# Second block: head sums, spreads and decay rows in row and column groups, key products by head pairs, value projection first, blocks stored sooner

## The chip, the cores and the metric

One core of one Trainium2 chip runs the kernel. The metric is the device time of one execution in microseconds (us). Times are medians of runs; the profile is of one execution, taken by the hardware profiler. The engines are TensorE (PE, its weight loads PEld), VectorE (DVE), ScalarE (ACT), GpSimd (POOL) and SyncE, whose queue (SP) issues the DMAs.

## What is computed

Two transformer blocks, one after the other, on 256 tokens of width 1024, in fp32. The first block has two layers of mixers, cross attention and MLP. The second block has a hybrid mixer (a grouped-query attention beside a gated delta rule in both directions) and an expert layer of 16 experts. The change is within the hybrid mixer:

```python
proj = h @ w_in
aq, ak, av, dq, dk, dv, dz, b_raw, a_raw, g_raw = split(proj)
q = axial_rope(rmsnorm_2(heads(aq, 8), q_norm_w)); k = axial_rope(rmsnorm_2(heads(ak, 2), k_norm_w))
attn = block_attention(q, k, heads(av, 2))
cq, ck, cv = split(silu(short_conv(concat([dq, dk, dv]), conv_w)))
qd, kd = l2norm(heads(cq, 8)) * 64 ** -0.5, l2norm(heads(ck, 8))
beta, g = sigmoid(b_raw), -exp(a_log) * softplus(a_raw + dt_bias)
# both directions, each with chunks of 128 tokens, per head:
gc = cumsum(g)
decay = exp(where(incl, gc[:, None] - gc[None, :], -inf))
L = where(strict, (kd * beta) @ kd.T * decay, 0)
T = inverse(eye + L)
u, w = T @ (v * beta), T @ (kd * beta * exp(gc))
a_intra = where(incl, qd @ kd.T * decay, 0)
...
dn = rmsnorm_2(o_fwd + o_bwd, dn_norm_w) * silu(dz)
merged = sigmoid(gate_a) * (attn @ w_attn_up) + sigmoid(gate_d) * (dn @ w_dn_up)
x = x + gt1 * (merged @ w_o)
```

## The kernel before

The program writes out the order of each engine's work by hand; engines wait for each other by semaphores. Activations lie with features on the 128 partitions and the 256 tokens along the free axis, so two heads of 64 share a 128-row chunk. Dense weights come in units of 2 MB through a ring of six slots: `take()` on PE waits for the next unit's load, and SP issues a unit's load when the unit that had the slot has been read (`unit_read`). Eight PSUM banks: `fill(name, b)` takes a bank (without `b` the next of banks 0 to 3) and waits until its last content was freed; `mark` tells that it is filled, `full` waits for that on another engine, `copied` waits until the content was read. All PE products of `mm` have line 521 of the profile, all ScalarE work has line 1719. An fp32 product of the program is two matmul instructions.

The part of the mixer that matters, in PE's order before: `ba` (beta and decay inputs); projections `dq` and `aq`; `gc` (the cumulated decays with tokens on partitions); `head_sums` for l2 (sums of squares of each of 16 heads, one 128x16 product for each of eight chunks, all into 16 rows of one bank); `ak`; `head_spread` for l2 (each head's inverse root, a row of 16, spread over its 64 rows by products 16x64); `av`; then for each of eight heads `triangle(h)`: `kk` (keys by keys and queries by keys, four products 64x128 with 128 columns) and `gr` (the head's cumulated decay as a row, in all 128 partitions, four products 128x128 with 128 columns), with a quarter of the projections `dv` and `dz` after each head. Then the sums and spreads of the attention's q and k norm (`qn`), gates 0 to 2, the rotation products (`rotg`), and the attention (`gqa`), with gates 3 to 6 between its heads. After it come the merging of the inverses (`X5` to `TT6`), the states and outputs of the delta rule, the attention up-projection (`au`), with the sums and spread of the output norm (`on`) between its groups, and the down branch (`du`).

On DVE, `differences(h)` subtracts the decays, `triangle(h)` multiplies kk, decay and beta; four convolutions of the value channels lie between the heads. `store_blocks` on SP waits for the last two heads' kk to be read, stores the 32x32 diagonal blocks, and loads them back; DVE then solves all blocks at once by 31 steps of forward substitution (`substitute`, L3016 and L3018), nine before the rotations and the others (`solve`) between the heads of the attention. `load_inverses` on SP (L1578) waits for that, stores both forms of the inverses and loads them to their places. SP's queue is strictly in order: before, the blocks are stored after unit GATES_AT+1 was issued, and the inverses before unit GATES_AT+4. GATES_AT is the first unit of the gate projections; GATES_AT+3 holds gates 6 and 7, GATES_AT+4 the attention up-projection. Expert units follow all dense units in SP's queue, but for one that is loaded early; the last dense unit waits until PE has read `au3`.

Lines of the kernel before: `head_sums` L1242, `head_spread` L1250, PE's `triangle` L1269, `store_blocks` L1568, `load_inverses` L1578, ScalarE's `head_root` L2024, DVE's `differences` L2969 and `triangle` L2978, `substitute` L3012, `solve` L3031.

Of the kernel before, what the change touches and what calls it, by code (L numbers as in the profile page):

```python
# [13 lines left out]
P = 128  # L14
S = 256
# [98 lines left out]
def dense_units(a):  # L114
# [49 lines left out]
def program(nc, a, out, plan):  # L164

    ctx = ExitStack()
    with ctx:
# [114 lines left out]
        dk_shift, g16 = small(4), small(16)  # L282
# [173 lines left out]
        QROOT, QINV = rtp[0:16, 512:768], rtp[0:16, 768:1024]  # L456
# [29 lines left out]
        def _(pe):  # L486
# [746 lines left out]
            columns("aq", hT)  # L1233
# [16 lines left out]
            def head_spread(tag, order, inverse, count, b=None):  # L1250

                pe.wait_ge(inv_ready, count)
                for r in order:
                    ps = fill(f"{tag}{r}", None if b is None else b + r)
                    for j in range(2):
                        c = 2 * (2 * r + j)
                        for i in range(2):
                            last = mm(ps[half(i), j * S:(j + 1) * S], ident[0:16, c + i:c + i + 1].broadcast_to([16, HD]),
                                      inverse, True, True)
                    mark(last, f"{tag}{r}")  # L1260
# [8 lines left out]
            def triangle(h):  # L1269

                r, c = half(h), h // 2
                ps = fill(f"kk{h}", 4 + 2 * (h % 2))
                for t in range(TT):
                    tok = slice(t * P, (t + 1) * P)
                    mm(ps[:, t * P:(t + 1) * P], cv[r, 4 + c, tok], cv[r, 4 + c, tok], True, True)
                    last = mm(ps[:, (2 + t) * P:(3 + t) * P], cv[r, 4 + c, tok], cv[r, c, tok], True, True)
                mark(last, f"kk{h}")
                ps = fill(f"gr{h}", 5 + 2 * (h % 2))
                for d in range(2):
                    for t in range(TT):  # L1280
                        j = 2 * d + t
                        last = mm(ps[:, j * P:(j + 1) * P],
                                  gl[:, t, 8 * d + h:8 * d + h + 1].broadcast_to([P, P]), cum[:, d, :], True, True)
                mark(last, f"gr{h}")

            copied(pe, *(f"l2{r}" for r in range(4)))
            for i, tag in enumerate(("dv", "dz")):
                w, u = take()
                for c in range(4):
                    triangle(4 * i + c)  # L1290
                    b, j = divmod(c, 2)
                    if j == 0:
                        ps = fill(f"{tag}{b}")
                    for k in range(DC):
                        last = mm(ps[:, j * S:(j + 1) * S], w[:, k, c * P:(c + 1) * P], hT[:, k, :], k == 0, k == DC - 1)
                    if j:
                        mark(last, f"{tag}{b}", u=u if b else None)
# [1975 lines left out]
```

## Time and profile before

| | |
|---|---|
| median of 3 runs | 1628.72 us (1624.97 to 1629.79) |
| the profiled execution | 1628.91 us |
| its span, first to last instruction | 1627.1 us |
| granted TensorE clock, mean of the span | 0.952 of full speed |
| busy PE, PEld, DVE, ACT, POOL | 1470.3, 1147.7, 767.4, 293.1, 30.0 us |
| matmuls | 10036 |
| moved by DMA | 396.51 MB, mean 244 GB/s |

Busy time is the union of an engine's instructions. Matmuls are pipelined, so one instruction's duration (some 380 ns for 256 columns) is longer than the step from one start to the next; costs are therefore read from starts. A granted clock of 0.5 is TensorE's lower level. A stretch's DMA share is the mean busy share of the core's 16 DMA engines. The mixer of the second block runs from about 885 to 1137 us of the span, the expert layer from about 1165 us on.

### The profile page before, as it was taken

The numbers are of one execution on the slowest core, as the hardware profiler recorded it, in microseconds if no ns is written. First come the engines' busy times: TensorE is split into PE (matmuls) and PEld (weight loads), VectorE is DVE, ScalarE is ACT, GpSimd is POOL, SyncE is SP. The second block draws the span as 40 slices with busy tenths as digits, with TensorE's granted clock in tenths as the row PEclk, the third lists the DMA queues.
The fourth block names the chain that finished last, engine by engine and source line by source line (L and its number), as shares of the span: only waits on it lengthen the run. The fifth ranks groups of instructions, "written<-read, shape, count | busy, mean of one in ns | idle before, by whom it ended". The sixth has DMA issues, their size and how long they took to land.

```text
span 1627.1 us, 23549 instructions
## 1 busy us (share of the span) xinstructions
PE 1470.3 (90%) x10036; PEld 1147.7 (71%) x10036; DVE 767.4 (47%) x1564; ACT 293.1 (18%) x735; POOL 30.0 (2%) x51
## 2 busy tenths in 40 slices
PE   9999999999999999999999999999997656666665
PEld 8779989998897899899988887778853212213111
DVE  6538618778586565287876837823231000000000
ACT  1331012310043411223101322231010001000000
POOL 0000000000001000000000012000000000000000
PEclk9999999999999999999999999999999888888778
DMA  9525415866344154257773004233999999999998
GB/s 395 217 79 207 155 53 220 315 257 257 142 155 156 61 198 156 82 216 286 279 290 143 1 1 130 104 105 113 385 405 429 427 429 428 426 430 428 427 430 332
DMA packets 47176, 396.51 MB, mean 244 GB/s; under 512 B 16352, under 2 KB 20192, under 8 KB 22624
## 3 DMA queue, kind: packets, MB, share of 16 engines
q1 hardware_dynamic: 45600, 393.51, 60.4%
q8 instruction: 80, 1.31, 0.3%
q10 hardware_dynamic: 1472, 1.49, 0.3%
q14 instruction: 24, 0.20, 0.0%
HBM read 392.36 MB, written 2.63 MB: 243 GB/s over the span
## 4 chain that ended last, share of the span: by engine, by line
PE 76%; DMA 21%; SPq 1%; DVE 1%; ACT 0%; issue 0%; DVEq 0%; ACTq 0%
PE pb L521 34%; DMA arena<-in_w_experts 16%; PE pb L1086 12%; PE pb L1050 11%; PE pb L621 7%; DMA ring<-in_w_experts 5%; PE pb L961 5%; PE pb L994 3%; PE pb L1135 2%; PE pb L889 1%; PE pb L1161 1%; PE pb L692 1%; SPq L1660 1%; PE pb L750 0%; DMA cols<-in_cols 0%
## 5 line engine op out<-in xcount | busy, mean ns | idle before, releaser
L521 PE MATMUL pb<-hT,ring 128*128 128x256 f32 x768 | 175.3, 384 | 0.0
L521 PE MATMUL pb<-ring,hT 128*32 128x512 f32 (+2 forms) x704 | 117.3, 701 | 53.3 <-DMA ring<-in_w_experts 52.1
L521 PEld LDWEIGHTS pb<-hT,ring 128*128 128x128 f32 x768 | 144.3, 191 | 26.1 <-issue 7.5
L3182 DVE SCALAR_TENSOR_TENSOR side<-side,pb 128x256 f32<-128x256 f32 x16 | 6.7, 421 | 272.2 <-ACT side L1719 272.2
L521 PEld LDWEIGHTS pb<-ring,hT 128*32 128x32 f32 (+1 forms) x704 | 35.6, 138 | 121.2 <-issue 64.6
L621 PE MATMUL pb<-arena,ring 128*128 128x256 f32 x512 | 118.2, 382 | 0.0
L1719 ACT ACTIVATE arena<-pb 128x512 f32<-128x512 f32 (+4 forms) x124 | 54.8, 457 | 322.0 <-PE pb L521 125.8
L621 PEld LDWEIGHTS pb<-arena,ring 128*128 128x128 f32 x512 | 94.9, 190 | 14.6 <-issue 2.9
L1719 ACT ACTIVATE side<-pb 128x256 f32<-128x256 f32 (+2 forms) x58 | 23.1, 406 | 417.0 <-PE pb L521 400.8
L521 PE MATMUL pb<-arena,hT 128*32 128x512 f32 x248 | 41.9, 796 | 33.5 <-DMA arena<-in_w_experts 20.5
L521 PE MATMUL pb<-arena 128*64 128x128 f32 (+4 forms) x464 | 69.8, 331 | 0.8 <-ACT arena L1719 0.8
L521 PEld LDWEIGHTS pb<-arena 128*64 128x64 f32 (+2 forms) x464 | 49.5, 168 | 18.8 <-issue 13.8
L2519 DVE CUSTOM_DVE_ANT_0 ring<-ring,arena,cols 128x1024 f32<-128x1024 f32 x48 | 59.2, 1278 | 0.0
L1086 PE MATMUL pb<-ring,arena 128*128 128x256 f32 x256 | 58.2, 379 | 0.0
L1086 PE MATMUL pb<-arena,hT 128*128 128x256 f32 x256 | 57.9, 379 | 0.0
L1086 PE MATMUL pb<-ring,hT 128*128 128x256 f32 x256 | 57.9, 379 | 0.0
L3194 DVE TENSOR_TENSOR side<-pb,rstd 128x256 f32<-128x256 f32 x16 | 6.8, 425 | 107.3 <-PE pb L521 107.3
L521 PE MATMUL pb<-ring,side 128*32 128x256 f32 x576 | 43.8, 456 | 14.8 <-DMA ring<-in_w_experts 10.0
L1050 PE MATMUL pb<-hT,ring 128*128 128x128 f32 x448 | 54.6, 275 | 0.0
L521 PEld LDWEIGHTS pb<-arena,hT 128*32 128x32 f32 x248 | 7.4, 126 | 66.0 <-DMA arena<-in_w_experts 33.5
L1086 PEld LDWEIGHTS pb<-arena,hT 128*128 128x128 f32 x256 | 48.6, 190 | 6.6
L1086 PEld LDWEIGHTS pb<-ring,hT 128*128 128x128 f32 x256 | 48.6, 190 | 6.6
(463 smaller groups left out, 2522.8 us busy)
## 6 DMA issues: line engine op xcount, KB each, us to landing
ring<-in_w_dense SPq DMA_DIRECT2D x85, 2048.0 KB, 7.9
ring<-in_w_experts SPq DMA_DIRECT2D x56, 2048.0 KB, 44.9
arena<-in_w_experts SPq DMA_DIRECT2D x18, 2048.0 KB, 44.0
extra<-in_w_experts SPq DMA_DIRECT2D x10, 2048.0 KB, 44.4
arena<-in_w_experts SPq DMA_DIRECT2D x9, 1024.0 KB, 41.8
cons<-in_w_experts SPq DMA_DIRECT2D x9, 1024.0 KB, 44.6
ring<-in_w_dense SPq DMA_DIRECT2D x2, 1536.0 KB, 6.6
ring<-in_w_dense SPq DMA_DIRECT2D x4, 512.0 KB, 8.6
```

The source lines that it names most:

```text
L521: return nc.tensor.matmul(o, l, r, start=st, stop=sp)
L621: last = nc.tensor.matmul(proj["banks"][c // 2][:, (c % 2) * S:(c % 2 + 1) * S], w[:, k, (c % 4) * P:(c % 4 + 1) * P], yT[:, k, :], start= ...
L692: last = nc.tensor.transpose(ps[:, c:c + P], pr2[:, n % 4, qb, kb * P:(kb + 1) * P], ident)
L889: last = nc.tensor.matmul(ps[b][:, j * S:(j + 1) * S], w[:, k, (2 * b + j) * P:(2 * b + j + 1) * P], raw_x[:, k, :], start=k == 0 and j == ...
L961: last = nc.tensor.matmul(ps[b][:, o:o + P], lhs[x][:, k, f * P:(f + 1) * P], rhs[x][:, k, :], start=x in "156" and f == 0 and k == 0, sto ...
L994: last = nc.tensor.matmul(pv[j[0]][:, FEAT[j[1]]], rows_[l](k), cols_[r](k), start=k == 0 and n < 4, stop=k == 3, skip_group_check=True)
L1050: last = nc.tensor.matmul(ps[b][:, o:o + P], lhs[x][:, k, f * P:(f + 1) * P], rhs[x][:, k, :], start=x in "156" and f == 0 and k == 0, sto ...
L1086: last = nc.tensor.matmul(pq[j[0]][:, FEAT[j[1]]], rows_[l](k), cols_[r](k), start=g == 0 and k == 0 and n < 4, stop=g == 3 and k == 3, sk ...
L1135: last = nc.tensor.matmul(ps[b][:, o:o + P], lhs[x][:, k, f * P:(f + 1) * P], rhs[x][:, k, :], start=x in "156" and f == 0 and k == 0, sto ...
L1161: last = nc.tensor.matmul(pv[b][:, FEAT[side_]], rows_[l][:, k, :], cols_[r][:, k, :], start=k == 0 and n < 4, stop=k == 3, skip_group_che ...
L1719: return nc.scalar.activation(o, i, f, **kw)
L2519: ins = V.tensor_tensor_reduce(out=w, in0=w, in1=c_row, scale=1.0, scalar=col("b_ada", 4 * i + f), op0=ALU.mult, op1=ALU.add, accum_out=mo ...
```

## The change

Order of the units: the value unit (`dv`, column 1792) is loaded and used before `aq` (column 0) and `kv`. On PE:
- `gcrow`: eight products make the cumulated decays of all heads and both directions as rows, in partitions 0 to 15 and again in 64 to 79. ScalarE copies them to SBUF (`decays`). A head's row is then spread by two products of 16 rows with 256 columns, for two heads in turn, one at rows 0 to 15 and one at rows 64 to 79 (`decay_rows`), where each head had four products of 128 rows.
- `triangles(p, ...)`: kk of a pair of heads, one in rows 0 to 63 and one in rows 64 to 127, in turn.
- `head_sums`: each pair of chunks has its own 32 output rows (a column group), the first chunks of all pairs ahead of the second. `head_spread`: inverses lie in rows of 32 for each pair; products of 32 rows by 64, row groups in turn.
- The order becomes dq, half of dv, gc, gcrow, half of dv, then aq in quarters with the decay rows, l2 sums and spread between, then aq, ak with the triangles, av, dz in quarters with the qn sums and spread.

ScalarE gets a small Sqrt ahead of each head root and a small Exp after it (`warms`), and does the exponentials of the decays earlier. DVE does the differences before and around the l2 normalisation, then all triangles, then the convolutions of the values; substitution steps 0 to 5 stand before the rotations, 6 to 17 before the attention, 18 to 30 in four parts behind its first four heads (before: 0 to 8, then five parts). GpSimd waits for the normalised keys before its first product. SP stores the blocks after unit GATES_AT, and stores and loads the inverses before unit GATES_AT+3.

```diff
-    for c0 in (1280, 768, 0):
+    for c0 in (1280, 768, 1792, 0):
         unit(a["w_in_2"], 0, D, c0, 512)
     unit(a["w_kv_2"], 0, D, 0, 384)
-    for c0 in (1792, 2304):
-        unit(a["w_in_2"], 0, D, c0, 512)
+    unit(a["w_in_2"], 0, D, 2304, 512)
...
             columns("dq", hT)
-            columns("aq", hT)
...
+            w, u = take()
+            quarter("dv", w, 0)
+            quarter("dv", w, 1)
             pe.wait_ge(g_ready, 1)
             ps = fill("gc")
...
+            ps = fill("gcrow")
+            for d in range(2):
+                for t in range(TT):
+                    for e in range(2):
+                        at_ = (2 * d + t) * P
+                        last = mm(ps[HD * e:HD * e + NE, at_:at_ + P], gl[:, t, :], cum[:, d, :], True, True)
+            mark(last, "gcrow")
+            quarter("dv", w, 2)
+            quarter("dv", w, 3, u)
...
-                for i, (c, sq_, count) in enumerate(chunks):
+                for c, sq_, count in sorted(chunks, key=lambda x: x[0] % 2):
+                    r, j = divmod(c, 2)
                     pe.wait_ge(l2_sq, count)
-                    last = mm(ps[0:16, 0:S], ehd[:, c, :], sq_, i == 0, i == len(chunks) - 1)
+                    last = nc.tensor.matmul(ps[quad(r), 0:S], ehd[:, j:j + 2, :].rearrange("p a b -> p (a b)"), sq_,
+                                            start=j == 0, stop=j == 1, skip_group_check=True)
...
+                ps = [fill(f"{tag}{r}", b) for r, b in zip(order, banks)]
+                for j in range(2):
+                    for i in range(2):
+                        for n, r in enumerate(order):
+                            pick = 32 * r + 2 * j + i
+                            last = mm(ps[n][half(i), j * S:(j + 1) * S], ident[quad(r), pick:pick + 1].broadcast_to([32, HD]),
+                                      inverse[quad(r), :], True, True)
...
+            def decay_rows(p, banks):
+
+                ps = [fill(f"gr{2 * p + e}", banks[e]) for e in range(2)]
+                for d in range(2):
+                    for e in range(2):
+                        pick = HD * e + 8 * d + 2 * p + e
+                        rows_ = slice(HD * e, HD * e + NE)
+                        last = mm(ps[e][:, 2 * d * P:2 * (d + 1) * P], ident[rows_, pick:pick + 1].broadcast_to([NE, P]),
+                                  decays[rows_, 2 * d * P:2 * (d + 1) * P], True, True)
...
+            def triangles(p, banks):
+
+                ps = [fill(f"kk{2 * p + e}", banks[e]) for e in range(2)]
+                for t in range(TT):
+                    tok = slice(t * P, (t + 1) * P)
+                    for at_, other in ((t, 4 + p), (2 + t, p)):
+                        for e in range(2):
+                            last = mm(ps[e][:, at_ * P:(at_ + 1) * P], cv[half(e), 4 + p, tok], cv[half(e), other, tok], True, True)
...
+            copied(pe, "gcrow")
+            decay_rows(0, (6, 7))
             head_sums("l2", ...)
+            decay_rows(1, (4, 5))
             w, u = take()
-            twice("ak", w)
-            head_spread("l2", (2, 3, 0, 1), rs[0:16, :], 1)
+            quarter("aq", w, 0)
+            decay_rows(2, (6, 7))
+            quarter("aq", w, 1)
+            head_spread("l2", (2, 3, 0, 1), rs, 1, (None, None, 4, 5))
+            decay_rows(3, (6, 7))
+            quarter("aq", w, 2)
+            copied(pe, *(f"l2{r}" for r in range(4)))
+            triangles(0, (4, 5))
+            quarter("aq", w, 3, u)
+            triangles(1, (6, 7))
+            w, u = take()
+            twice("ak", w, lambda: triangles(2, (4, 5)))
+            triangles(3, (6, 7))
             rows("av", hT, w, u, 2 * P, P)
...
+            w, u = take()
+            quarter("dz", w, 0)
+            head_sums("qn", ..., 4)
+            quarter("dz", w, 1)
+            head_spread("qn", range(3), QINV, 2, (5, 6, 7))
+            quarter("dz", w, 2)
+            quarter("dz", w, 3, u)
             gates(0, 0, 1)
-            head_spread("qn", range(3), QINV, 2)
-            gates(1, 0, 1)
             for r in range(3):
                 copied(pe, f"qn{r}")
...
+            gates(1, 0, 1)
             gates(2, 0, 1)
...
-                    head_spread("on", range(2), rs[0:16, :], 3, 5)
+                    head_spread("on", range(2), rs, 3, (5, 6))
...
-                if u == GATES_AT + 4:
+                if u == GATES_AT + 3:
                     load_inverses()
...
-                if u == GATES_AT + 1:
+                if u == GATES_AT:
                     store_blocks()
...
+            copied(pool, *(f"l2{r}" for r in range(4)))
...
+                fn(warms[:, 2 * w_:2 * w_ + 1], eps, ACT.Sqrt)
                 ps, free = full(act, f"{tag}_sum")
-                fn(dst, ps[0:16, 0:S], ACT.Sqrt, scale=scale, bias=eps[0:16, :]).then_inc(free, 1)
+                fn(dst[0:32 * n, :], ps[0:32 * n, 0:S], ACT.Sqrt, scale=scale, bias=eps[0:32 * n, :]).then_inc(free, 1)
+                fn(warms[:, 2 * w_ + 1:2 * w_ + 2], eps, ACT.Exp)
...
+            copy("dv0", cp[:, 8:10, 2:2 + S], pairs)
+            ps, free = full(act, "gcrow")
+            for e in range(2):
+                rows_ = slice(HD * e, HD * e + NE)
+                ins = fn(decays[rows_, :], ps[rows_, :], ACT.Copy)
...
             differences(0)
+            differences(1)
+            head_inverse("l2", rs, rt, 4)
+            for h in range(2, 6):
+                differences(h)
+            for r in (2, 3, 0, 1):
+                ps, free = full(dve, f"l2{r}")
...
+            differences(6)
+            differences(7)
             for h in range(8):
-                if h + 1 < 8:
-                    differences(h + 1)
                 triangle(h)
-                if h in (2, 3, 5, 6):
-                    convolve((0, 0, 8, 9, 0, 10, 11)[h])
...
+            convolve(8)
+            head_inverse("qn", QINV, QROOT, 3)
+            convolve(9)
...
+            convolve(10)
+            convolve(11)
...
-            for j in range(9):
+            for j in range(6):
                 substitute(j)
...
+            silu(2)
+            for j in range(6, 18):
+                substitute(j)
...
-                for j in range(9 + 22 * min(h, 5) // 5, 9 + 22 * min(h + 1, 5) // 5):
+                for j in range(18 + 13 * min(h, 4) // 4, 18 + 13 * min(h + 1, 4) // 4):
                     substitute(j)
-                if h == 4:
+                if h == 3:
```

## Rows read from the trace of the kernel before

**Rows 1.** Stretches: length, busy (instructions) PE, PEld, DVE, ACT, POOL; clock; DMA.

```profile
904.80:1036.00 131.20, 131.20 (x676) 107.46 (x675) 85.62 (x217) 33.03 (x71) 17.70 (x34) 0.96 0.17 57
1036.00:1136.40 100.40, 99.14 (x1008) 79.08 (x1007) 43.47 (x105) 28.45 (x64) 2.94 (x3) 0.98 0.32 106
1136.40:1200.00 63.60, 63.47 (x354) 53.79 (x353) 22.66 (x55) 9.17 (x24) 0.00 (x0) 0.97 0.91 375
1200.00:1627.00 427.00, 277.60 (x2446) 100.98 (x2444) 29.06 (x69) 25.61 (x74) 0.00 (x0) 0.84 0.99 419
947.80:954.60 6.80, 6.80 (x33) 6.07 (x30) 0.93 (x2) 0.28 (x1) 0.00 (x0) 0.51 0.00 0
1012.60:1015.80 3.20, 3.20 (x9) 2.45 (x8) 1.94 (x3) 0.00 (x0) 0.87 (x1) 0.50 0.50 148
```

**Rows 2.** SP's queue in order of time: start, us, line, DMAs issued.

```profile
1004.16 7.06 SPq L1573 DMA_DIRECT2D blocks<-ring  x8
...
1059.64 0.33 SPq L1581 DMA_DIRECT2D inverses<-arena  x1
...
1071.85 0.49 SPq L1656 DMA_DIRECT2D ring<-in_w_dense  x1
...
1136.61 0.33 SPq L1656 DMA_DIRECT2D ring<-in_w_dense  x1
```

**Rows 3.** TensorE in order of time: start, us, form, instructions merged.

```profile
904.79 27.87 PE L521 MATMUL pb<-hT,ring 128*128 128x256 f32 x128
...
988.87 1.16 PE L521 MATMUL pb<-arena 64*128 64x128 f32 x8
989.95 1.16 PE L521 MATMUL pb<-cons,sml 128*128 128x128 f32 x8
...
1035.52 0.60 PE L750 MATMUL pb<-cons,arena 128*128 128x128 f32 x4
...
1069.86 1.99 PE L521 MATMUL pb<-hT,ring 128*128 128x256 f32 x8
```

**Rows 4.** TensorE's products by form, 885 to 1137: gr, kk, spreads, sums, spreads of qn.

```profile
L521 PE MATMUL pb<-cons,sml 128*128 128x128 f32 x64 | 9.3, 287 | 0.0
L521 PE MATMUL pb<-arena 64*128 64x128 f32 x64 | 9.2, 285 | 0.0
...
L521 PE MATMUL pb<-rstd,cons 16*64 16x256 f32 x48 | 6.0, 399 | 0.0
L521 PE MATMUL pb<-arena,cons 128*16 128x256 f32 x24 | 5.5, 380 | 0.0
...
L521 PE MATMUL pb<-root_pairs,cons 16*64 16x256 f32 x24 | 3.0, 391 | 0.0
```

**Rows 5.** TensorE elsewhere: pairs of heads in fox; expert products of groups.

```profile
98.01 0.39 PE L521 MATMUL pb<-arena,cons 64*128 64x128 f32 x4
98.24 0.60 PE L521 MATMUL pb<-arena 64*128 64x256 f32 x4
...
1210.41 1.91 PE L521 MATMUL pb<-arena,side 128*32 128x256 f32 x32
...
1212.93 1.17 PE L855 MATMUL pb<-side 32*128 32x256 f32 x16 [0.61 <-DVE side L3194]
```

**Rows 6.** ScalarE at the router: its root, and the table load behind.

```profile
1183.15 0.26 ACT L1719 ACTIVATE sml<-pb,cons 128x2 f32<-128x2 f32 x1 [1.67 <-PE pb L1483]
1183.43 1.28 ACT L1719 ACT_TABLE_LOAD   x1
```

**Rows 7.** VectorE: substitution's first line (min/median/max ns); first maxima and scaling.

```profile
L3016 DVE TENSOR_TENSOR arena<-arena x31: 193/357/425, 1018.3 to 1058.1; 128x31 f32<-128x31 f32 x2, 128x60 f32<-128x60 f32 x2, 128x87 f32<-128x87 f32 x2, 128x112 f32<-128x112 f32 x2
...
1032.05 1.29 DVE L2262 TENSOR_REDUCE sml<-pb 128x2 f32<-128x512 f32 x2 [1.72 <-PE pb L521]
...
1034.03 0.62 DVE L2270 TENSOR_SCALAR arena<-arena,sml 128x256 f32<-128x256 f32 x2
```

**Rows 8.** DMA issues of the page: KB each, median us to landing.

```profile
ring<-in_w_dense SPq DMA_DIRECT2D x85, 2048.0 KB, 7.9
```

More of the change, by code:

```diff
@@ L1232, in _, with quarter @@
             columns("dq", hT)
-            columns("aq", hT)
+            piece = [None]
+            def quarter(tag, w, c, u=None):
+                b, j = divmod(c, 2)
+                if j == 0:
+                    piece[0] = fill(f"{tag}{b}")
+                for k in range(DC):
+                    last = mm(piece[0][:, j * S:(j + 1) * S], w[:, k, c * P:(c + 1) * P], hT[:, k, :], k == 0, k == DC - 1)
+                if j:
+                    mark(last, f"{tag}{b}", u=u if b else None)
+            w, u = take()
+            quarter("dv", w, 0)
+            quarter("dv", w, 1)
             pe.wait_ge(g_ready, 1)
@@ L1246, in head_sums, with head_spread @@
                     pe.wait_ge(l2_sq, count)
-                    last = mm(ps[0:16, 0:S], ehd[:, c, :], sq_, i == 0, i == len(chunks) - 1)
+                    last = nc.tensor.matmul(ps[quad(r), 0:S], ehd[:, j:j + 2, :].rearrange("p a b -> p (a b)"), sq_,
+                                            start=j == 0, stop=j == 1, skip_group_check=True)
                 mark(last, f"{tag}_sum")
-            def head_spread(tag, order, inverse, count, b=None):
+            def head_spread(tag, order, inverse, count, banks):
@@ L1252, in head_spread @@
                 pe.wait_ge(inv_ready, count)
[L1253 to L1260, printed above, removed]
+                ps = [fill(f"{tag}{r}", b) for r, b in zip(order, banks)]
@@ L1286, in _ @@
[L1286 to L1297, printed above, removed]
@@ L1299, in _ @@
-            head_sums("qn", [(c, gsq[:, c, :], 5 + c // 2) for c in range(4)] + [(4 + g, gksq[:, g, :], 7) for g in range(2)])
+            quarter("aq", w, 0)
[8 more added lines that the diff above has]
+            triangles(1, (6, 7))
@@ L2045, in _ @@
             silu_tanh(0)
-            copy("dq0", cp[:, 0:2, 2:2 + S], pairs)
+            for i in range(2):
+                copy(f"dq{i}", cp[:, 2 * i:2 * i + 2, 2:2 + S], pairs)
             act.wait_ge(cvs_ready, 1)
@@ L2055, in _, with decay @@
                 head_squares(sqk[:, 4 + 2 * r:6 + 2 * r, :], cv[:, 2 * r:2 * r + 2, :])
-            copy("aq1", gq[:, 2:4, :], pairs)
-            for r in range(2):
-                copied(act, f"aq{r}")
-                head_squares(gsq[:, 2 * r:2 * r + 2, :], gq[:, 2 * r:2 * r + 2, :])
-            head_root("l2", rt[0:16, :], 0.25)
-            for g in range(2):
-                copy(f"ak{g}", gk[:, g, :], lambda ps: ps[:, 0:S])
-            copied(act, "ak0", "ak1")
-            head_squares(gksq, gk)
-            act.wait_ge(ekd_ready, 1)
-            fn(ekd, ekd, ACT.Exp).then_inc(ekx_ready, 1)
-            for t in range(TT):
-                copy(f"av{t}", gv[:, t, :], lambda ps: ps[:, 0:P])
-            for h in range(8):
+            head_root("l2", rt, 4, 0.25, 0)
+            copy("dv1", cp[:, 10:12, 2:2 + S], pairs)
+            def decay(h):
                 r, c = half(h), h // 2
@@ L2078, in _ @@
                 ins.then_inc(free, 1)
-                if h in (1, 3):
-                    copy(f"dv{h // 2}", cp[:, 7 + h:9 + h, 2:2 + S], pairs)
-                if h in (5, 7):
-                    i = h // 2 - 2
-                    ps, _ = full(act, f"dz{i}")
-                    fn(dzt[:, 2 * i:2 * i + 2, :], pairs(ps), ACT.Tanh, scale=0.5).then_inc(dzt_ready, 1)
-            head_root("qn", QROOT, 1.0 / HD)
+            for h in range(6):
+                decay(h)
+            copy("aq0", gq[:, 0:2, :], pairs)
+            decay(6)
+            decay(7)
+            copy("aq1", gq[:, 2:4, :], pairs)
+            for r in range(2):
+                copied(act, f"aq{r}")
+                head_squares(gsq[:, 2 * r:2 * r + 2, :], gq[:, 2 * r:2 * r + 2, :])
+            for g in range(2):
+                copy(f"ak{g}", gk[:, g, :], lambda ps: ps[:, 0:S])
+            copied(act, "ak0", "ak1")
+            head_squares(gksq, gk)
+            head_root("qn", QROOT, 3, 1.0 / HD, 1)
+            act.wait_ge(ekd_ready, 1)
+            fn(ekd, ekd, ACT.Exp).then_inc(ekx_ready, 1)
+            for t in range(TT):
+                copy(f"av{t}", gv[:, t, :], lambda ps: ps[:, 0:P])
+            for i in range(2):
+                ps, _ = full(act, f"dz{i}")
+                fn(dzt[:, 2 * i:2 * i + 2, :], pairs(ps), ACT.Tanh, scale=0.5).then_inc(dzt_ready, 1)
             gates(0)
```

61 lines of the change are left out of this document (24 added, 37 removed).

## The prediction

> **What bounds the kernel now.** I read the windows by stage first. From 904.8 to 1036 us TensorE is busy 131.20 of 131.20 us, from 1036 to 1136.4 us 99.14 of 100.40; VectorE has 85.62 and 43.47 us of work there, ScalarE 33.03 and 28.45, and the DMA engines are nearly idle (share 0.17 and 0.32). From 1136.4 us on it is the other way round: the DMA share is 0.91, then 0.99 to the end, and TensorE is busy 277.60 of 427 us [rows 1]. So the mixer of the second block, which the change rewrites, is bound by TensorE alone, and what follows by the stream of expert weights. Next SP's queue: the last dense unit goes out at 1136.61 us, when TensorE has read the third group of the attention up-projection, and the expert units are queued behind it [rows 2]. The stream is of fixed length, about 490 us, so a microsecond that TensorE saves before 1136.6 is a microsecond off the end. The narrow products come third: they are what the change touches, and TensorE runs them one after the other or two at a time. The granted clock comes last: 0.51 for 6.8 us after the first spread and 0.50 for 3.2 us after the second [rows 1], the lower of TensorE's levels (1.2 against 2.4 GHz).
>
> The profiled execution took 1628.91 us (span 1627.1), against the median 1628.72, so I count from 1628.9.
>
> **Unit of cost.** Each fp32 product is two instructions. 128 wide ones of 256 columns take 27.87 us [rows 3], 0.217 us each; 128 columns are then 0.109.
>
> **Decay rows (gr).** 64 instructions, 9.3 us with their tails [rows 4]; by starts one head takes about 1.0, so 8.0. Now: 16 instructions of 128 columns make all rows at once (gcrow), alternating two column halves, and 32 of 256 columns with 16 rows each alternate two row groups. The fox stage of this kernel has such pairs: four instructions of 64x128 start at 98.01 and the next work at 98.24, 0.058 each, and four of 64x256 take 0.60 with their tail, where one after another they would take 0.87 [rows 5]. So pairs run at half the unit: 32 x 0.109 = 3.5, 16 x 0.055 = 0.9, and 0.1 for each of five changes of form: 4.8. Gain 3.2; without overlap 32 x 0.217 + 16 x 0.109 = 8.7, a loss of 0.7.
>
> **Key products (kk).** One head's eight instructions take 989.95 - 988.87 = 1.08 us [rows 3], 8.7 for all (9.2 with tails, [rows 4]). Taken by head pairs, 16 x 0.055 + 0.1 = 0.95, four times 3.8. Gain 4.9; nothing without overlap. These eight run at 0.135 each, above the 0.109 of their columns, so something besides the columns paces them; in fox the same form went at 0.058 in pairs, hence I take the pair price. The Trainium skill speaks against this: TensorE: Matmul & The Clock Gate, section LDWEIGHTS, has a weight load cost its columns over 1.2, 107 ns for 128, whatever the rows; 16 loads in a row would be 1.7 us for a pair, an estimate from that page, and the gain 1.9. By that rule four fox instructions would need 0.43; the trace shows 0.23 [rows 5] and does not agree.
>
> **Head sums.** 36 instructions (l2 16, qn 12, on 8); the 24 of l2 and on take 5.5 [rows 4], so all about 8.1 by starts. Now each pair of chunks has its own column group of 32. The experts have that form: 32 instructions 128x256 of four column groups in 1.91 us [rows 5], 0.06 each. l2 is then 1.0, qn and on with four instructions in line in each group 0.9 to 1.0 too: 2.9. Gain 5.2, nothing at worst.
>
> **Head spreads.** 72 instructions, 6.0 + 3.0 us [rows 4], 8.8 by starts: already two at a time. Now four, three and two row groups by two column halves. No row shows both splits at once. Four row groups: 16 instructions in 1.17 us [rows 5]. If all tiles overlap, 0.9 each; if only four at a time, 1.75. I take 1.4, 1.3, 1.1: nearer the row with four, a little better. Sum 3.8, gain 5.0 (3.5 to 6.2; nothing at worst).
>
> **Clock.** The two stretches cost 6.8 x 0.49 + 3.2 x 0.50 = 4.9 us, 0.3 of it already in the spreads. Both follow spreads of 3 and 4 us of narrow work. Now narrow pieces are 1 to 3 us long between projections of 3.5 us. I expect both gone and allow one shorter drop elsewhere with a chance of four in ten: 4.6 - 0.6 = 4.0.
>
> **What moves.** The value projection comes before the query projection, so that the decays run on ScalarE and VectorE while TensorE is on wide work. I laid the new order out by hand with these durations. TensorE's new waits: for the copied gcrow (ScalarE writes it 5 us before it is wanted), and for banks 6 and 7 before the third pair of decay rows, which arrive within 0.1 us of the last exponential of the second head. Behind that wait stands all of TensorE; a slip of ScalarE is paid one for one, 0 to 1 us, and I take 0. VectorE inverts, multiplies and does its triangles ahead of need. GpSimd now waits for the normalised keys too, about 950 us; its eight heads are wanted only after 1100. Table loads: ScalarE gains a load before the router's root, 1.28 us, where it now idles 1.67 [rows 6]; price nothing, 1.3 at most if the idle went.
>
> **Blocks stored sooner.** The triangles end at about 969 us, and the stores, now at 1004.16 [rows 2], go out at 970, behind the gate unit's load, and the blocks are back near 984. VectorE can only use them after its last convolution, 985.9, as those need the late projection products. So the gain of 34 us in the store becomes some 31 us at the solver's start (1018.3 to 1058.1 now, [rows 7]), more than TensorE moves up.
>
> Two new stalls come out of it. First, VectorE: after the rotation product (993.6 in my order) it has three rotations (6.2), the dz gates (1.3), silu (1.2) and substitution steps 6 to 17, two instructions each of up to 0.425 us, 10.4 in all: until 1012.7. Only then does it take the first head's maximum. Maximum, exponential and scaling now go from 1032.05 to 1034.65 [rows 7]; 2.6 makes 1015.3. TensorE has done scores and the half gate by 1013.8 and waits 1.4 us.
>
> Second, SP: the inverses are now stored and loaded ahead of gate unit GATES_AT+3 and no longer of +4. The remaining 13 steps hang on four heads' scaling; they end near 1032.2. The inverses' queue takes 1071.85 - 1059.64 = 12.2 us [rows 2], then the unit lands after 7.9 [rows 8]: 1052.3, with 0.1 for the release 1052.4. TensorE wants it when gate 6 begins, 34.3 us after the first turn (1035.52 and 1069.86, [rows 3]): 1015.3 + 34.3 = 1049.6. Stall 2.8, between 1.5 (the fastest landing would be earlier) and 4. Behind it stand two heads of attention and all that follows. Before, the unit left long before the inverses.
>
> **Sum.** 3.2 + 4.9 + 5.2 + 5.0 + 4.0 - 1.4 - 2.8 = 18.1 us off: 1628.9 - 18.1, about 1611 us.
>
> **The rivals.**
> *Full overlap, loads in time.* All tiles side by side give 20.5 in place of 18.3 for the four families, and the unit lands without a wait: 20.5 + 4.6 - 1.4 = 23.7, 1605 us. For it: the four-group rows; against: the order of SP's queue.
> *Weight loads pace the pairs.* The key products keep 0.135 per instruction because 128-column loads don't overlap: 4.9 less, 1616 us; with spreads and decay rows no better than two at a time as well, 3 to 4 less again, 1619. For it: 0.135 against 0.109 [rows 3]; against: the fox pairs. The page named above would give this side.
> *It doesn't do what it says*: narrow products run one at a time because changes of form cost what the overlap gives. Then only the clock is left and the stalls take it back: 0.6 + 4.0 - 4.2, 1628 us, no change. Every fox row speaks against it.
> *Slower: the clock falls for the whole stretch.* The new pieces fill an eighth to a half of the array, and from 935 to 986 us they stand between all projections. Each microsecond of work done at 1.2 GHz costs one more. If the 31 us from the first decay rows to the last key products ran so, the loss is 31 against the gain, 1628.9 - 18.1 + 31 = 1642. It decides from 18 us of work on, 36 us at half clock. For it: both drops now follow narrow work; against: each ended within 7 us, under wide products [rows 1], which are two thirds of the new stretch.
>
> **How the numbers follow.** Forecast 1611 (1607 to 1614): 0.55. Full overlap, 1605 (down to 1603): 0.14. Weight loads, 1615 to 1621: 0.18. No change: 0.08. Slower: 0.05. A measurement of this kernel tells about 0.3%, 5 us, from no change; the first three cases are faster by more: 0.87. The range runs from 1604, inside the second case, to 1621, the end of the third, and leaves the last two out.
>
> **What would show it.** gcrow once, then four pairs of decay rows of about 0.95 us and four of key products likewise; three sums near 1 us; spreads of 1 to 1.5; clock 1.0 from 935 to 1010; the block stores near 970; a wait of TensorE for a scaled row near 1014, and one for a dense unit's load near 1050; the last dense unit near 1118. The prediction is wrong in a step if key pairs take over 1.5 us, if the clock is 0.5 for over 10 us in the stretch, if the gate unit comes without a wait, and wrong as a whole if the last dense unit leaves after 1131 us.

## The result, and the profile after

| | before | after |
|---|---|---|
| median, measured side by side | 1626.85 us (4 runs) | 1616.19 us (4 runs, 1612.95 to 1617.2) |
| ratio | | 0.9927 [0.9912, 0.9942] |
| the profiled execution (span) | 1628.91 (1627.1) | 1616.32 (1614.5) |

The change takes 12.6 us off between the two profiled executions, and 10.7 between the medians. The forecast was 18.1, 1611 us in place of 1616: the time lies inside the range, but 5 us of the sum did not come. The table follows TensorE through the mixer (us from the start of the span).

| | before | after | moved | forecast |
|---|---|---|---|---|
| first turn of the weights could begin | 1035.52 | 1015.67 | -19.9 | -21.7 |
| it begins, after the wait for VectorE | 1035.52 | 1017.01 | -18.5 | -20.2 |
| gate 6 begins | 1069.86 | 1057.33 | -12.5 | -17.5 |
| merging of the inverses (X5) begins | 1080.06 | 1070.32 | -9.7 | |
| last dense unit leaves | 1136.61 | 1123.82 | -12.8 | -18.6 |

So nearly 20 us are won by the attention, 10 of them are lost within the attention, and 3 come back behind it. TensorE's timeline of after shows the first part; it answers to [rows 3] and [rows 4] (start, us, form, instructions merged, and in brackets the idle time and what ended it).

```profile
926.91 1.06 PE L521 MATMUL pb<-cons,sml 128*16 128x128 f32 x16
927.90 7.17 PE L521 MATMUL pb<-hT,ring 128*128 128x256 f32 x32
935.01 1.13 PE L521 MATMUL pb<-ring,cons 16*128 16x256 f32 x8
936.07 1.07 PE L1271 MATMUL pb<-arena,cons 128*32 128x256 f32 x16
937.07 1.13 PE L521 MATMUL pb<-ring,cons 16*128 16x256 f32 x8
938.13 3.72 PE L521 MATMUL pb<-hT,ring 128*128 128x256 f32 x16
941.78 1.13 PE L521 MATMUL pb<-ring,cons 16*128 16x256 f32 x8
...
946.50 1.12 PE L521 MATMUL pb<-rstd,cons 32*64 32x256 f32 x32
947.54 1.13 PE L521 MATMUL pb<-ring,cons 16*128 16x256 f32 x8
948.61 3.72 PE L521 MATMUL pb<-hT,ring 128*128 128x256 f32 x16
952.26 1.16 PE L521 MATMUL pb<-arena 64*128 64x128 f32 x16
953.35 3.72 PE L521 MATMUL pb<-hT,ring 128*128 128x256 f32 x16
```

By starts: gcrow 0.99 us, a pair of decay rows 1.06, the l2 sums 1.00, the l2 spreads 1.04, a pair of key products 1.09. A wide quarter (a quarter of a projection, 16 instructions) between two such pieces takes 3.65 (938.13 to 941.78). At the step of the 128 wide ones of [rows 3], whose successor starts at 932.50, it would be 3.46. Behind the decay rows of before it took 3.55, to the 988.87 of [rows 3]:

```profile
985.32 3.62 PE L521 MATMUL pb<-hT,ring 128*128 128x256 f32 x16
```

The second part is in the waits of TensorE from 900 to 1130 us (us in total, times, the longest), in the timeline around them, and in the windows of those stretches (length, then PE, PEld, DVE, ACT, POOL, granted clock, DMA share).

```profile
PE pb L521 <- DMA ring<-in_w_dense: 4.2, 1, 4.2
...
PE pb L750 <- DVE arena L2320: 1.3, 1, 1.3
```

```profile
1017.01 0.66 PE L750 MATMUL pb<-cons,arena 128*128 128x128 f32 x4 [1.34 <-DVE arena L2320]
...
1018.65 1.97 PE L521 MATMUL pb<-arena 128*64 128x256 f32 x4
1020.55 2.73 PE L521 MATMUL pb<-hT,ring 128*128 128x256 f32 x8
...
1026.63 1.08 PE L521 MATMUL pb<-arena 128*64 128x256 f32 x4
1027.63 1.99 PE L521 MATMUL pb<-hT,ring 128*128 128x256 f32 x8
...
1057.33 3.78 PE L521 MATMUL pb<-hT,ring 128*128 128x256 f32 x8 [4.23 <-DMA ring<-in_w_dense]
1060.90 1.06 PE L750 MATMUL pb<-cons,arena 128*128 128x128 f32 x4
```

```profile
1018.65:1023.11 4.46, 4.46 (x13) 2.87 (x13) 4.18 (x12) 1.02 (x4) 0.00 (x0) 0.62 0.00 0
...
1057.33:1062.60 5.27, 5.27 (x14) 4.28 (x15) 0.00 (x0) 0.60 (x1) 0.00 (x0) 0.50 0.68 289
...
944.90:1010.80 65.90, 65.90 (x410) 53.93 (x408) 50.10 (x119) 14.25 (x31) 13.51 (x33) 1.00 0.34 112
```

Two waits, both foreseen, and behind each a granted clock of 0.5 to 0.62, which was not: products that take 1.00 and 1.83 us by starts elsewhere take 1.90 and 2.56 from 1018.65, 1.6 lost by these starts and 1.7 by the window's clock (4.46 us at 0.62). From 1057.33 gate 6 takes 3.57 for 1.83, and with the two pieces behind it 2.8 us are lost. Before, the clock was low behind the spreads [rows 1]; now it is 1.00 through all of that stretch. SP's queue shows where the second wait is from (start, us, line, DMAs merged).

```profile
971.87 9.03 SPq L1610 DMA_DIRECT2D blocks<-ring  x8
982.46 0.51 SPq L1612 DMA_DIRECT2D arena<-blocks  x1
...
1035.80 0.33 SPq L1618 DMA_DIRECT2D inverses<-arena  x1
...
1049.11 75.04 SPq L1693 DMA_DIRECT2D ring<-in_w_dense  x5
```

The blocks are stored from 971.87 and loaded from 982.46, close to the forecast's 970 and 984. The unit of gates 6 and 7 leaves at 1049.11, 13.3 us after the first store of the inverses, and is there at 1057.33, 8.2 us later.

Of what comes back behind the attention, 1.7 us are the sums and spread of the output norm. The rest was not in the forecast: in the states' stage, one projection of eight wide instructions ran at the low clock before and at the full one after (first fence before, second after): by starts 3.29 and 1.83 us, 1.5 less.

```profile
1108.44 3.46 PE L521 MATMUL pb<-side,ring 128*128 128x256 f32 x8
1111.73 3.68 PE L521 MATMUL pb<-arena,ring 128*128 128x64 f32 x32
```

```profile
1098.81 1.99 PE L521 MATMUL pb<-side,ring 128*128 128x256 f32 x8
1100.64 3.68 PE L521 MATMUL pb<-arena,ring 128*128 128x64 f32 x32
```

### The profile page after: what moved, and what is told of

The parts are those of the page before. It is cut to its first block, busy times and chain, and to the rows that moved or that the text cites. A ratio compares the mean times of both kernels' runs of the same rounds, so it can differ in the third digit from the quotient of the medians.

```text
span 1614.5 us, 23539 instructions
## 1 busy us (share of the span) xinstructions
PE 1449.5 (90%) x10020; PEld 1131.3 (70%) x10020; DVE 765.8 (47%) x1564; ACT 297.7 (18%) x745; POOL 29.3 (2%) x51
## 4 chain that ended last, share of the span: by engine, by line
PE 73%; DMA 23%; DVE 2%; SPq 1%; issue 1%; ACT 1%; DVEq 0%; ACTq 0%
PE pb L521 30%; DMA arena<-in_w_experts 14%; PE pb L1086 12%; PE pb L1050 11%; DMA ring<-in_w_experts 8%; PE pb L621 7%; PE pb L961 5%; PE pb L994 3%; PE pb L1135 2%; PE pb L889 1%; PE pb L1161 1%; PE pb L692 1%; DMA ring<-in_w_dense 1%; DMA cols<-in_cols 0%; PE pb L750 0%
## 5 line engine op out<-in xcount | busy, mean ns | idle before, releaser
L521 PE MATMUL pb<-ring,hT 128*32 128x512 f32 (+2 forms) x704 | 109.9, 666 | 47.8 <-DMA ring<-in_w_experts 46.5
L521 PE MATMUL pb<-ring,side 128*32 128x256 f32 x576 | 51.9, 522 | 18.4 <-DMA ring<-in_w_experts 14.6
L521 PE MATMUL pb<-arena 128*64 128x128 f32 (+4 forms) x464 | 66.1, 333 | 0.8 <-ACT arena L1757 0.8
L521 PEld LDWEIGHTS pb<-arena 128*64 128x64 f32 (+2 forms) x464 | 46.0, 169 | 17.9 <-issue 13.1
```

Of the source, the lines that this page charges most:

```text
L521: return nc.tensor.matmul(o, l, r, start=st, stop=sp)
```

## The experiments

Each starts from the changed kernel. Positions are compared with the profile of after.

**The baseline again**, on one chip with the next three kernels (before there: 1627.33 us).

> The changed kernel once more, beside the others of this call. It took 1616.2 us (ratio to before 0.9927). In its trace TensorE waits 4.23 us for the load of unit GATES_AT+3 at 1053, 1.34 us for the first scaled row at 1015.7, and its clock falls after both waits. Expected here: 1616 us, ratio 0.991 to 0.994, the same two waits within 0.5 us.

1615.83 us, ratio 0.9933 [0.992, 0.9945]; the same two waits, 4.2 and 1.3 us, and a low clock behind both.

**The inverses one unit later in SP's queue**, as before.

```diff
-                if u == GATES_AT + 3:
+                if u == GATES_AT + 4:
                     load_inverses()
```

> The changed kernel with the inverses stored and loaded before unit GATES_AT+4 again, as before the change; nothing else differs. Theory: the queue order alone makes the wait of 4.23 us, and the waiting makes the clock fall after it (about 2.9 us of lost work between 1057 and 1062). Then both go: 7.1 us less than the changed kernel, about 1609 us, ratio to before 0.988 to 0.990. Rival A: the clock falls there because of the attention's narrow products; then only 4.2 us go, 1612 us. Rival B: the merging of the inverses or the expert stream is the next bound and takes the gain back; then 1615 to 1616 us, with a wait of TensorE ahead of the X5 products or a later start of the expert loads relative to the last dense unit.

1608.06 us, ratio 0.9889 [0.9875, 0.9904], 7.8 less than the baseline. Gate 6, which now begins without a wait:

```profile
1051.45 1.99 PE L521 MATMUL pb<-hT,ring 128*128 128x256 f32 x8
```

The wait of 4.2 us and the low clock behind it are gone, and no wait for the inverses has come in their place. This one line of the change costs it 4.2 + 2.8 us; the remaining 0.8 lies inside the spread of the runs. (In this profile the clock also stayed up behind the first wait; of that more below.)

**The wait filled with products.** Nine products of 128x256 on constants are issued where TensorE would stand; the order of SP's queue stays as changed.

```diff
-                    if n % 2 == 0:
+                    if n == 6:
+                        gate_unit[1] = fill(f"sg{n // 2}_{n % 2}", b)
+                        for _ in range(9):
+                            mm(gate_unit[1][:, 0:S], ident, view(cons, CONS["cum"][0], S), True, True)
...
                         gate_unit[0] = take()
```

> The changed kernel with nine products of 128x256 on constants ahead of the wait for unit GATES_AT+3 (into the bank that gate 6 overwrites; nothing is left out of the computation). They take 9 x 0.434 = 3.9 us, a little less than the wait of 4.23. Theory: the clock falls after the wait because TensorE stands still; with the wait filled the clock stays at full and 2.9 us are saved though nothing else is faster: about 1613 us, ratio to before 0.991. Rival: the clock follows the narrow products of the attention and not the wait; then it still falls between 1057 and 1062 and the time stays at 1616 us.

1613.21 us, ratio 0.9915 [0.99, 0.993], 2.6 less than the baseline:

```profile
1051.39 4.15 PE L521 MATMUL pb<-cons 128*128 128x256 f32 x18
1056.10 1.99 PE L521 MATMUL pb<-hT,ring 128*128 128x256 f32 x8 [0.56 <-DMA ring<-in_w_dense]
1057.93 0.60 PE L756 MATMUL pb<-cons,arena 128*128 128x128 f32 x4
```

```profile
1056.10:1062.60 6.50, 6.50 (x31) 5.06 (x32) 0.00 (x0) 0.60 (x1) 0.00 (x0) 1.00 0.51 217
```

The unit still lands 4.7 us after TensorE would have begun to wait (1051.39 to 1056.10), but gate 6 now takes 1.83 us by starts and not 3.57. So here the low clock follows TensorE's standing still, not the DMA traffic or the attention's own products.

**The substitution split otherwise as well**: seven steps ahead of the attention in place of twelve, and the rest in five parts, with the inverses behind GATES_AT+4.

```diff
-            for j in range(6, 18):
+            for j in range(6, 13):
...
-                for j in range(18 + 13 * min(h, 4) // 4, 18 + 13 * min(h + 1, 4) // 4):
+                for j in range(13 + 18 * min(h, 5) // 5, 13 + 18 * min(h + 1, 5) // 5):
...
-                if h == 3:
+                if h == 4:
```

> As the one with the inverses before GATES_AT+4, and in addition the substitution steps 13 to 17 moved from before the attention to behind its heads (6 to 12 before it, 13 to 30 in five parts). Theory: the wait of 1.34 us for the first scaled row comes from VectorE's steps ahead of the first maximum, and the clock's fall after it costs another 1.7 us; both go, 3 us less than with the inverses alone, about 1606 us, ratio to before 0.986 to 0.988. Rival: the steps between the heads make VectorE late for a later head, or the inverses come back after TensorE reaches the X5 products (it has some 5 us of room by the trace); then no gain or a loss of up to 3 us against the other.

1607.14 us, ratio 0.9885 [0.9869, 0.9901]; the first turn begins at 1015.72 without a wait. It is 0.9 below the run with the inverses alone, where 3 were expected, and the intervals overlap: a further gain is not shown. The wait of 1.34 went, but the low clock that I had added to its price did not always follow it: of eleven profiles with that wait, five show it behind (after and the baseline among them), six do not, the run with the inverses alone among these. Behind the second wait it fell in all nine profiles that have one of 2.7 to 4.8 us. By its median this is the fastest version, 20 us under before.

**The block stores late again.**

```diff
-                if u == GATES_AT:
+                if u == GATES_AT + 1:
                     store_blocks()
```

> The changed kernel with the block stores put back behind the gate unit GATES_AT+1, as before; all else as changed. Theory (the early store is a part that carries others): the unit ahead of the stores is held by TensorE's progress, so the stores leave about 17 us later than the 971.87 of the changed kernel and the blocks are back near 1001 instead of 983 to 987. VectorE's step that needs them then stands with the rotations, silu and twelve substitution steps behind it, so the scaled first row is 11 to 14 us late: TensorE waits that long near the first turn, 1627 to 1630 us in all. Rival (the early store only moves a transfer that had slack): no wait over 3 us, 1616 us.

1629.21 us beside 1628.13 for the kernel before, one run each: the whole gain is gone. SP's queue, VectorE's step that needs the blocks, and TensorE:

```profile
971.30 16.57 SPq L1693 DMA_DIRECT2D ring<-in_w_dense  x2
987.97 9.55 SPq L1610 DMA_DIRECT2D blocks<-ring  x8
```

```profile
1003.66 1.04 DVE L3070 COPY arena<-arena 64x1024 f32<-64x1024 f32 x1 [16.45 <-DMA arena<-blocks]
```

```profile
1015.16 8.59 PE L521 MATMUL pb<-hT,ring 128*128 128x256 f32 x32 [11.27 <-DVE arena L3081]
```

TensorE's next gate waits 11.27 us for a PSUM bank. What frees it is VectorE's multiplication with `dz` (L3081), and that stands behind the copy, six steps and the rotations in VectorE's queue. So in the new order the early store is a condition: without it the time that TensorE saves is spent in this wait. Whether the early store alone would speed up the kernel before was not run.

**The order of a pair's key products**: head by head (eight instructions of one row group, then eight of the other), and by fours. Diff of the first; in the second the loop over heads stands between those over `t` and `at_`.

```diff
-                for t in range(TT):
+                for e in range(2):
...
-                        for e in range(2):
+                    for t in range(TT):
```

> The changed kernel with the key products of a pair issued one head after the other (eight instructions of one row group, then eight of the other) instead of alternating. Theory (two row groups overlap only where neighbours in the queue differ): 16 instructions take 2.2 us a pair as before, instead of 1.09, and 4.4 us are lost in all, some of it swallowed by the 4.2 us wait for the dense unit: start of the attention 4.4 us later, the end 0 to 4.4 us later. Rival (row groups work from queues of their own, and the order does not matter): 1.1 us a pair, no change. A third reading, by the Trainium skill's page TensorE: Matmul & The Clock Gate, section LDWEIGHTS, would have 1.7 us a pair in either order.

> The changed kernel with the key products of a pair issued four instructions to a row group at a time, where the changed kernel alternates after two and the head-by-head order after eight. Theory (work for the other row group is taken up while a few instructions wait for their own, so that four in line cost little, as in the spreads by row group with four in line for each tile, and eight cost 0.55 us): 1.1 to 1.2 us a pair. Rival (the cost grows evenly with the run: each instruction that stands in line beyond the first pair costs its share): 1.25 to 1.35 us.

First pair and the work behind it, head by head, then by fours:

```profile
952.15 1.71 PE L521 MATMUL pb<-arena 64*128 64x128 f32 x16
953.79 3.72 PE L521 MATMUL pb<-hT,ring 128*128 128x256 f32 x16
```

```profile
951.91 1.26 PE L521 MATMUL pb<-arena 64*128 64x128 f32 x16
953.11 3.72 PE L521 MATMUL pb<-hT,ring 128*128 128x256 f32 x16
```

1.64, 1.20 and, alternating after two, 1.09 us: neither the 2.2 of the one theory nor the 1.1 of the other for runs of eight, and 1.20 at the upper edge of what was expected for runs of four. The steps, 0.11 from two to four and 0.44 from four to eight, fit one delay per piece, 0.109 for each instruction by which a run is longer than three; that is a fit to three points. The times (1616.14 and 1615.17 us, one run each) do not tell them from the baseline: the 2.2 us of the first met an execution in which no low clock followed the wait for VectorE.

**The spreads row group by row group.**

```diff
-                for j in range(2):
-                    for i in range(2):
-                        for n, r in enumerate(order):
+                for n, r in enumerate(order):
+                    for j in range(2):
+                        for i in range(2):
```

> The changed kernel with the head spreads issued one row group after the other, so that neighbours in the queue share their 32 rows and differ in the column half alone: the same products at the same places, two tiles at a time instead of eight. Theory (two at a time, and what clocks TensorE down is narrow work that leaves most of the array idle, as with the decay rows issued four times): 32 instructions by 0.109 and 0.2 for the change of form make 3.5 to 3.7 us for the first spreads instead of 1.04, the granted clock falls to 0.5 behind them as behind the spreads of the kernel before, and the wide quarter that follows takes about 5.4 us instead of 3.7; the attention starts 4 to 5 us later. Rival (row groups overlap whatever the order, or the clock fell behind the decay rows for their 16 rows only): 1.0 to 2 us, or 3.6 us at an unbroken clock of 1.00.

```profile
946.81 1.16 PE L521 MATMUL pb<-rstd,cons 32*64 32x256 f32 x32
947.90 1.13 PE L521 MATMUL pb<-ring,cons 16*128 16x256 f32 x8
```

1.09 us and a clock of 1.00 behind it (1617.15 in all): the theory falls. Eight instructions of a row group stand in line here, four for each of its two tiles, and the row groups still overlap.

**Narrow work made longer**, to see what it costs without its ends and behind which of it the clock falls. Each repeats products with the same result: the l2 spreads four times (eight tiles of 32x64), one pair of decay rows four times (two tiles of 16x128), and the first row group of the l2 spreads four times more (two tiles of 32x64).

```diff
+                for z in range(4 if tag == "l2" else 1):
...
+                times = 4 if p == 1 else 1
+                for z in range(times):
...
+                for z, j, i in [(z, j, i) for z in range(5 if tag == "l2" else 1) for j in range(2) for i in range(2)]:
...
+                        for n, r in enumerate(order if z == 0 else order[:1]):
```

> The changed kernel with the 32 products of the first head spreads issued four times over, 128 in place of 32, all eight tiles of 32 rows by 64 columns in use. Before, 4 us of spreads in two tiles of 16 rows by 64 columns were followed by a granted clock of 0.51. Theory A (the clock falls after narrow work of some length, however much of the array it holds): a stretch of 0.5 behind these 4.2 us. Theory B (what counts is how much of the array is in use; all of its tiles are): the clock stays 1.00 and the start of the attention is only the added 3.1 us later.

> The changed kernel with one pair of decay rows issued four times over, 32 instructions in place of 8, two tiles of 16 rows by 128 columns in use, 4.2 us in place of 1.06. Theory A (length of the narrow work): granted clock 0.5 behind it, as behind the spreads of the kernel before. Theory B (rows and columns held, a quarter of the array's columns times rows): as these hold few rows, 0.5 here and 1.00 in the run with the spreads. Theory C (the clock fell before for another reason): 1.00 in both.

> The changed kernel with the products of the first row group of the first head spreads issued four times more, 32 further instructions that use two tiles of 32 rows by 64 columns, behind the 32 of all eight tiles. Theory (the clock falls behind narrow work that leaves most of the array idle, whatever its operation): the piece takes 1.04 + 32 by 0.109 = 4.5 us, 3.5 of it in two tiles, and the granted clock is 0.5 for some microseconds behind it, as behind the decay rows issued four times and not as behind the spreads of all tiles issued four times. Rival (it falls behind the decay rows for something else in them, such as their 16 rows or their 128 columns): 4.5 us and a clock of 1.00.

The three timelines in that order, the first and the third with a window behind the narrow work:

```profile
946.32 3.71 PE L521 MATMUL pb<-rstd,cons 32*64 32x256 f32 x128
949.96 1.13 PE L521 MATMUL pb<-ring,cons 16*128 16x256 f32 x8
951.02 3.72 PE L521 MATMUL pb<-hT,ring 128*128 128x256 f32 x16
...
950.00:954.00 4.00, 4.00 (x27) 3.29 (x23) 3.91 (x10) 0.30 (x1) 1.13 (x3) 1.00 0.00 0
```

```profile
936.88 3.72 PE L521 MATMUL pb<-ring,cons 16*128 16x256 f32 x32
940.53 5.41 PE L521 MATMUL pb<-hT,ring 128*128 128x256 f32 x16
945.87 1.13 PE L521 MATMUL pb<-ring,cons 16*128 16x256 f32 x8
```

```profile
948.28 4.55 PE L521 MATMUL pb<-rstd,cons 32*64 32x256 f32 x64
952.77 1.63 PE L521 MATMUL pb<-ring,cons 16*128 16x256 f32 x8
954.32 6.56 PE L521 MATMUL pb<-hT,ring 128*128 128x256 f32 x16
960.81 1.16 PE L521 MATMUL pb<-arena 64*128 64x128 f32 x16
...
955.00:960.00 5.00, 5.00 (x13) 3.97 (x12) 2.42 (x9) 2.02 (x6) 3.91 (x10) 0.50 0.00 0
```

The first two pieces are equally long, 3.64 and 3.65 us. Behind the eight tiles the wide quarter takes its 3.65 by starts and the granted clock stays at 1.00; behind the two tiles it takes 5.34, and behind the third kernel's two tiles 6.49, with a granted clock of 0.50 from 955 to 960 us. Length alone does not tell them apart, nor does the operation: the clock fell behind both that worked two tiles at a time, as it did behind the spreads of before [rows 1, 4], and not behind the one with eight. Each is one execution, and as the clock behind the first wait differs from one to the next, this is what these three showed and not proof for every execution. (In all 1620.18, 1620.9 and 1619.94 us, with the repeated work in them.) The same rows give the price of a form: 96 more spread instructions take 2.60 us, 0.027 each, an eighth of the 0.217 of [rows 3]; so of the 1.04 for 32 some 0.17 is left as a fixed part of the piece, which I take for the change of form. For decay rows 24 more take 2.59, 0.108 each, and 0.20 is left.

## Why the prediction was right or wrong

**What bounds the kernel** was right: all that TensorE kept until the last dense unit left came off the end (-12.8 at 1123.82, -12.6 in all).

**The narrow products** were right in sum. Gains measured by starts, with the forecast: decay rows 2.7 (3.2), key products 4.3 (4.9), sums 5.1 (5.2), spreads 5.7 (5.0): 17.8 for 18.3. In that the errors offset each other: the spreads, at 1.03 each, came out near the 0.9 of all tiles side by side, and the other three gained less than forecast. The Trainium skill's rule for weight loads (TensorE: Matmul & The Clock Gate, LDWEIGHTS), 1.7 us for a pair of key products, does not agree with the 1.09 measured; only head by head, at 1.64, is the time near it. The same page of the Trainium skill (The mechanism) lets a load run ahead when the row groups differ, out of a queue 64 deep. The trace agrees on the first part: the 16 loads of the first pair take 0.97 us together, 0.061 each. On how far it reaches, eight in line already cost 0.55 us here.

**The changes of form** were mis-sized. I allowed 0.1 for each piece. The piece itself has a fixed part of 0.17 to 0.20, and the wide quarter behind it takes 3.65 where the bare step gives 3.46; behind the wide end I allowed nothing. The rows of before could have told: the eight key products of one head take 1.08 us, 0.21 above the 0.109 each of their columns [rows 3]. I read that as a slower pace of every instruction; a fixed part fits as well, and it fits the 1.09 of a pair too (16 by 0.055 and 0.2). Up to the first turn the families give 16.1 of the 19.9 us. The other 3.7 to 3.8 should have been the 4.6 of the low clock, so 0.9 went into longer wide pieces. With the 0.5 of the narrow ones this is 1.4 of the 1.9 us that the attention comes later than forecast; the rest lies in the order that I laid out by hand and stays open. The Trainium skill's page TensorEngine Tiling (Array Packing), Key Properties, says that a change of the tiling mode drains TensorE; the rows agree that each change costs something, and give a size.

**The clock** was right where I looked and wrong where I did not. Both low stretches of before are gone, 4.6 us, and the array stays at 1.00 through every narrow piece; the rival of a low clock for the whole stretch did not occur. But I priced the two new waits at their length. Behind them the clock fell too: 2.8 us behind the second, 1.7 behind the first in this execution; 1.5 came back in the states' stage, by a stretch that I had not counted. The term was 4.0 and came out at 4.6 + 1.5 - 1.7 - 2.8 = 1.6. For all such drops the sum held 0.6. Why it follows the wait of 1.3 us in some executions only is open.

**The first wait** was right: 1.34 for 1.4. VectorE's scaling is 1.7 us late and TensorE 1.9. VectorE's last steps start with TensorE's rotation product, so both were late together and the difference stayed.

**The second wait** had the right mechanism and the wrong size, 4.23 for 2.8. The inverses are stored at 1035.80, not 1032.2: 1.7 by the later attention and some 1.6 by the low clock behind the first wait. (In the run with the inverses one unit later the first scaled row is there at the same time, the clock stays up, and they are stored at 1034.21.) The queue took 13.3 for 12.2, the landing 8.2 for 7.9, 1.4 together; TensorE itself came 3.5 late. I chose one value for a difference of two long chains; it moved by all that moved one and not the other.

**The sum**: 18.1 - 0.5 (narrow pieces) - 0.9 (wide pieces) - 2.4 (clock) - 1.4 (second wait) + 0.1 (first) = 13.0, measured 12.8 at the last dense unit and 12.6 in all.

**The rivals.** The time is that of "weight loads pace the pairs" (1616), by coincidence: its reason was that the key products gain nothing, and they gained 4.3, a pair at 1.09 us. "Full overlap, loads in time" was near in its first half, though its 20.5 is not itemised (with spreads at 0.9 each the forecast's own terms come to 19.4); its other half is the run with the inverses one unit later, 1608 us, 3 above that rival's 1605. "It doesn't do what it says" falls with the pieces. What I had costed at nothing stayed so: no wait of TensorE for GpSimd appears, and ScalarE, with its added table loads, still idles 0.37 us ahead of the router's root, for 1.67 before [rows 6].

## What to carry to other kernels

Price a new wait of TensorE at its length plus what the clock may do behind it: here 4.2 us of standing cost 7, and 1.3 us cost 1.3 in some executions and 3 in others. When a step is moved forward in an ordered queue, look at what is queued behind it; one unit's place decided 8 of 20 us. Narrow products are cheap when they use many tiles at once, in runs of a few instructions for each tile, and gathered so that forms change seldom.

## What the runs showed of the hardware

- 32-row by 64-column tiles overlap eight at a time in fp32: 128 instructions of 256 columns in 3.64 us, 0.027 each, and full overlap does not need strict alternation: spreads issued row group by row group, four instructions for each tile, cost 0.05 us more in 32; key products with eight in line for a tile cost 0.55 more in 16.
- A narrow piece costs 0.17 to 0.20 us beside its instructions, and the wide quarter behind it 0.19 (3.65 for 3.46); behind the full-height decay rows of before that was 0.09. That both are the change of form is a reading, not shown apart.
- 3.65 us of work in two small tiles was followed by the lower clock level, 3.64 us in eight tiles was not, one execution each. Standing still for 2.7 to 4.8 us was followed by it in nine profiles of nine, for 1.3 us in five of eleven.
